# A hybrid decoder layer on one core: conditioning slices regrouped on VectorE, slot arithmetic moved ahead of the first expert, one table load and some dummy matmuls changed

## The reference

```python
c_act = silu(c)
sh1, sc1, gt1, sh2, sc2, gt2 = split(c_act @ w_ada + b_ada, 6)   # six rows of 1024
h = modulate(rmsnorm(x, norm1_g), sh1, sc1)
mix = hybrid_mixer(h, ...)       # 4 GLA heads (two to a unit), 4 HGRN2 heads (one to a unit), chunked
x = x + gt1 * mix
h2 = modulate(rmsnorm(x, norm2_g), sh2, sc2)
ffn = hierarchical_moe(h2, ...)  # 32 experts of width 256, best group of 4, best 2 of its 8 experts
x = x + gt2 * ffn
shf, scf = split(c_act @ w_ada_final + b_ada_final, 2)
out = modulate(rmsnorm(x, norm_f_g), shf, scf)
```

## Time and profile before

| | |
|---|---|
| median of 3 runs | 1039.96 us (1039.79 to 1043.06) |
| profiled execution | 1039.79 us |
| its span, first to last instruction | 1038.0 us |
| PE busy | 981.2 us, 95% |
| PE weight loads | 771.5 us, 74% |
| DVE busy | 797.5 us, 77% |
| ACT busy | 530.4 us, 51% |
| chain that ended last | PE 66%, DVE 15%, DMA 10%, ACT 4%, issue 3% |
| mean granted clock of PE | 0.992 |

### The profile page before, as it was taken

The page is one execution under the profiler, slowest core; times in us unless marked ns, Lnnn a source line. Parts: engine busy times, 40 slices in busy tenths (PEclk is TensorE's granted clock), DMA queues, the critical chain, the costliest instruction groups (busy, mean ns, idle before and its releaser), DMA issues.

```text
span 1038.0 us, 15568 instructions
## 1 busy us (share of the span) xinstructions
PE 981.2 (95%) x5698; PEld 771.5 (74%) x5698; DVE 797.5 (77%) x1486; ACT 530.4 (51%) x930; POOL 109.1 (11%) x151
## 2 busy tenths in 40 slices
PE   5899998999899999999999999899999999999996
PEld 5669688978897998989988888466666666666642
DVE  7859879836983886958676768898888888787828
ACT  4555532654275555555663323465665656565522
POOL 0201101000100000010010000121221221212100
PEclk9899999999999999999999999999999999999998
DMA  9823633232324233230185434589999999999375
GB/s 364 250 80 105 199 105 103 62 101 61 105 61 122 82 93 111 62 102 1 58 333 164 183 141 182 186 292 363 372 370 367 372 366 358 368 355 349 105 306 205
DMA packets 81033, 206.78 MB, mean 199 GB/s; under 512 B 11878, under 2 KB 40630, under 8 KB 72780
## 3 DMA queue, kind: packets, MB, share of 16 engines
q1 hardware_dynamic: 59232, 156.25, 41.8%
q0 software_dynamic: 15120, 43.72, 13.2%
q10 hardware_dynamic: 6620, 6.00, 1.8%
HBM read 189.61 MB, written 24.71 MB: 206 GB/s over the span
## 4 chain that ended last, share of the span: by engine, by line
PE 66%; DVE 15%; DMA 10%; ACT 4%; issue 3%; SPq 1%; ACTq 0%; DVEq 0%; POOLq 0%
PE PS L1999 13%; PE PS L2001 12%; PE PS L2000 12%; DMA WGU<-in_w_exp_up 7%; PE PS L2297 4%; PE PS L2083 3%; PE PS L2305 3%; PE PS L2303 3%; PE PS L2304 3%; DVE AT L1466 3%; PE PS L2288 2%; PE PS L2408 1%; DVE ACC L1264 1%; DMA AST<-in_w_ada 1%; PE PS L2133 1%
## 5 line engine op out<-in xcount | busy, mean ns | idle before, releaser
L1999 PE MATMUL PS<-WH,HT 128*128 128x256 f32 x512 | 146.8, 287 | 1.3 <-ACT GVH L924 1.3
L2000 PE MATMUL PS<-WL,HT 128*128 128x256 f32 x512 | 144.8, 283 | 0.0
L2001 PE MATMUL PS<-WH,HL 128*128 128x256 f32 x512 | 144.8, 283 | 0.0
L1825 DVE TENSOR_TENSOR WGL<-WGU,WGH 128x1024 fp32r<-128x1024 f32 x96 | 116.9, 1219 | 18.1 <-ACT WGH L1171 16.8
L1466 DVE COPY_PREDICATED AT<-MASK,PS 128x64 f32<-128x64 uint8 x320 | 72.8, 228 | 63.1 <-PE PS L2094 44.0
L1171 ACT ACTIVATE WGH<-WGU 128x1024 fp32r<-128x1024 f32 x96 | 98.5, 1064 | 33.6 <-DMA WGU<-in_w_exp_up 28.1
L1999 PEld LDWEIGHTS PS<-WH,HT 128*128 128x128 f32 x512 | 98.2, 192 | 4.0 <-issue 4.0
L2000 PEld LDWEIGHTS PS<-WL,HT 128*128 128x128 f32 x512 | 98.2, 192 | 0.0
L2001 PEld LDWEIGHTS PS<-WH,HL 128*128 128x128 f32 x512 | 98.1, 192 | 0.0
L2303 PE MATMUL PS<-WGH,XGTH 128*96 128x512 f32 x192 | 88.3, 460 | 0.0
L1863 DVE TENSOR_TENSOR WDL<-WDN,WDH 128x2048 fp32r<-128x2048 f32 x32 | 73.4, 2293 | 17.6 <-ACT WDH L1181 17.5
(11 more groups left out here) (355 smaller groups left out, 2259.0 us busy)
## 6 DMA issues: line engine op xcount, KB each, us to landing
WGU<-in_w_exp_gate SPq DMA_DIRECT2D x32, 1024.0 KB, 12.6
WGU<-in_w_exp_up SPq DMA_DIRECT2D x32, 1024.0 KB, 18.5
WDN<-in_w_exp_down SPq DMA_DIRECT2D x32, 1024.0 KB, 13.5
AR<-in_w_ada POOLq DMA_DIRECT2D x32, 512.0 KB, 4.2
WF<-in_w_in SPq DMA_DIRECT2D x28, 512.0 KB, 5.6
AST<-in_w_ada SPq DMA_DIRECT2D x16, 512.0 KB, 8.6
AR<-in_w_ada_final POOLq DMA_DIRECT2D x16, 512.0 KB, 4.7
YG<-expert_rows SPq DMA_DIRECT2D x8, 1024.0 KB, 12.3
```

Source lines behind the costliest of these rows:

```text
L1825: V.tensor_tensor(WGL[s][:, :, ks, :], WGU[s][:, :, ks, :], WGH[(NCH * s + c) % 4][:].bitcast(F32), ALU.subtract).then_inc(wgl_ready, 1)
L1999: MM(ps, wh, xh, start=first, stop=False)
L2000: MM(ps, wh, xl, start=False, stop=False)
L2001: return MM(ps, wl, xh, start=False, stop=last)
```

## The change

Five edits. (1) The slices are regrouped: 5 ahead of the decay, 3 ahead of the five `mul`, 4 inside `remaining(0)`, 4 ahead of the memsets, and 8 instead of 9 in the attention steps of unit 0; the total stays 48. (2) The Silu of one column on ACT is removed. (3) `extra_counts`, `extra_slots` and both picks (now `picked_slots`) stand ahead of the low parts of the first expert's weights; before, the counts and slots stood behind them and the picks inside expert steps 0 and 2. (4) `warm` reads row tile 0 of X1 instead of the last one. (5) The dummy matmuls ahead of the first expert rows are 8 instead of 7, and the 2 behind the transposes of these rows are removed.

```diff
--- before.py
+++ after.py
@@ -142,7 +142,7 @@
     UNIT_ADA = ["gt1", "sh2", "sc2", "gt2", "shf", "scf"]
 
     ROW_STEP = {0: 4, 1: 4}
-    SLICE_STEPS = {0: [1, 5, 5, 9, 9, 11, 11, 13, 13], 1: [5, 5, 9, 9, 11, 11, 13, 13],
+    SLICE_STEPS = {0: [5, 5, 9, 9, 11, 11, 13, 13], 1: [5, 5, 9, 9, 11, 11, 13, 13],
                    2: [0, 1, 6, 7], 3: [0, 1, 6, 7], 4: [], 5: []}
     SLICES_BETWEEN = {2: 4, 3: 4}
 
@@ -1198,7 +1198,6 @@
 
             for part in range(NCH):
                 weights_high(0, 0, part, True)
-            A(TOCK[:], RR[:, 0:1], ACT.Silu)
             rows_high(0, 0, True)
             for s in range(4):
                 expert_step(0, s, True, False)
@@ -1393,7 +1392,7 @@
             link(V.tensor_tensor(LBT[:, 0, :], LBT[:, 0, :], LB[:, 0, :], ALU.subtract))
             V.tensor_tensor(LBT[:, 1, :], LBT[:, 1, :], LB[:, 0, :], ALU.subtract).then_inc(consts, 1)
             lows(0, v_chunks(0))
-            for _ in range(4):
+            for _ in range(5):
                 unit_slice()
 
             def level(ap, s):
@@ -1521,16 +1520,12 @@
             link(V.tensor_scalar(LB[:, 1, :], LB[:, 0, :], -1.0, 1.0, ALU.mult, ALU.add))
             link(V.tensor_scalar(LB[:, 2, :], LB[:, 1, :], -1.0, None, ALU.mult))
             lows(1, k_chunks(1))
-            unit_slice()
             for i in range(NL):
                 sub(0, i)
-                if i in (1, NL - 1):
-                    unit_slice()
-            unit_slice()
+            for _ in range(KD - 5):
+                unit_slice()
             for i in range(NL):
                 mul(0, i)
-            unit_slice()
-
             def remaining(u):
                 sub(u, NL)
                 sub(u, NL + 1)
@@ -1538,23 +1533,21 @@
                     v_.wait_ge(pj_ready, number[("oT", 0, heads(0) - 1, 1)] + 1)
                 sub(u, NL + 2)
                 if u == 0:
-                    unit_slice()
-                    unit_slice()
+                    for _ in range(4):
+                        unit_slice()
                 for i in range(NL, ITEMS):
                     mul(u, i)
-                    if u == 0 and i == NL:
-                        unit_slice()
 
             remaining(0)
             for u in range(UNITS):
                 if is_gla(u):
                     lows(u, g_chunks(u))
+                    for _ in range(4 if u == 0 else 0):
+                        unit_slice()
                     link(V.memset(AT2[:], 0.0))
                     if u == 0:
                         link(V.memset(S[0][64:P], 0.0))
                         link(V.memset(S[1][0:64], 0.0))
-                        for _ in range(3):
-                            unit_slice()
                 later = decay_steps(u + 1) if u + 1 < UNITS else []
                 for n in range(first_step[u], first_step[u + 1]):
                     attention_step(n)
@@ -1737,6 +1730,15 @@
                 link(V.tensor_scalar(IDX[:, 0:NE], EM[0:C, 0, :], float(PAD), None, ALU.add))
                 V.tensor_single_scalar(IDXG[:, 0:NE], IDX[:, 0:NE], PLANE - 1, op=ALU.bitwise_and).then_inc(idxg_ready, 1)
 
+            def picked_slots(hs, dst):
+                for k, mk in enumerate((M1, M2)):
+                    link(V.tensor_tensor(EM[:, hs], SCR[:, hs], mk[:, hs], ALU.mult))
+                    link(V.tensor_reduce(V8[:, 7, hs], EM[:, hs], AX, ALU.add))
+                    last = V.tensor_copy(dst[:, k, hs], V8[:, 7, hs])
+                    if k == 0:
+                        link(last)
+                return last
+
             router_weights()
             v_.wait_ge(gt1_in, 48)
             v_.wait_ge(ios, 12)
@@ -1789,11 +1791,7 @@
                 link(V.tensor_tensor(SCR[:], SCR[:], bc_t(DX[:], NE, NT), ALU.mult))
                 link(V.tensor_tensor(SCR[:], SCR[:], RK[:], ALU.add))
                 link(V.tensor_tensor(SCR[:], SCR[:], bc_t(EC[:], NE, NT), ALU.add))
-
-            def picked_slot(k):
-                link(V.tensor_tensor(EM[:], SCR[:], (M1, M2)[k][:], ALU.mult))
-                link(V.tensor_reduce(V8[:, 7, :], EM[:], AX, ALU.add))
-                link(V.tensor_copy(SLOT[:, k, :], V8[:, 7, :]))
+                link(picked_slots(slice(0, NT), SLOT))
 
             def extra_experts():
                 link(V.tensor_tensor(CMP[:], XINC[0:1, :].rearrange("p (a e) -> p a e", a=1).to_broadcast([1, NX, NE]),
@@ -1870,13 +1868,13 @@
                 if more:
                     weights_low(*after, 2)
 
+            extra_counts()
+            extra_slots()
             for part in range(NCH):
                 weights_low(0, 0, part)
-            extra_counts()
             rows_low(0, 0)
-            extra_slots()
             for s in range(4):
-                expert_step(0, s, True, False, (lambda: picked_slot(s // 2),) if s in (0, 2) else ())
+                expert_step(0, s, True, False)
                 if s == 1:
                     v_.wait_ge(gt2_in, 16)
             with v_.Fori(1, NE // 4 - 1) as it:
@@ -2230,7 +2228,7 @@
 
             def warm(count):
                 for _ in range(count):
-                    MM(WB[0], IDENT[:], X1[:, NT - 1, 0:HALF], start=True, stop=True)
+                    MM(WB[0], IDENT[:], X1[:, 0, 0:HALF], start=True, stop=True)
 
             for kind, i, *part in out_order[1:]:
                 if kind == "rank" and i == 1:
@@ -2278,7 +2276,7 @@
                             last = MM(ps[:, 4 * NE:5 * NE], ONEB[:], MB[:, t * NE:(t + 1) * NE],
                                       start=(t == 0), stop=(t == NT - 1))
                     last.then_inc(pj_ready, 1)
-            warm(7)
+            warm(8)
             evacuated(("lg", NT - 1))
             evacuated(("rank", 1))
 
@@ -2359,7 +2357,6 @@
 
             pe.wait_ge(xg_in[0], 16)
             xg_transposes(0, t_ready)
-            warm(2)
             for s in range(4):
                 expert_step(0, s, True, False)
             with pe.Fori(1, NE // 4 - 1) as it:
```

## The result

The changed kernel takes 1053.39 us (median of 4), the kernel before 1041.28 us beside it: a ratio of 1.0108, 95% interval 1.0092 to 1.0126. It is slower by 1.1%, by 9.6 to 13.1 us as the interval has it. Three executions on record were far longer (1103.92 us here, 1223.93 us beside e1, 5515.1 us in e9); they count in the medians and not in the ratios. The forecast was 1058.0 us with a range of 1048.8 to 1062.4.

A forecast was written before the change was run, and what follows sets the result against it. PE, two thirds of the span, was taken as the bound, with DVE releasing it at both places. 1039.8 plus 9.1 + 3.5 + 2.9 - 1.1 + 0.3 + 3.5 = 18.2 gave 1058.0 us, range 1048.8 to 1062.4.

The forecast's parts named there:

- The slices' waits: Start of unit 0's attention: grouped slices make DVE wait for AR loads, first mask 9.1 us later.
- The clock in unit 0: PE returns at 1.2 GHz after its gap ahead of the second levels: +3.5 us, bounds 0 and 5.0.
- the walk: Slice-by-slice timing of DVE up to unit 0's first mask, giving 139.9 instead of 130.82.
- Small work ahead of the first low parts: Start of the experts: counts, slots and picks on DVE delay PE's transposes by 2.9 us.
- Pick and table load: Expert step 0: ATT 1.1 us earlier without the pick; Silu table load delays the first SIL, +0.3 us.
- The clock at the experts: PE idles 4.4 us ahead of the second transposes, then runs at 1.2 GHz: +3.5 us, up to 5.0.
- The dummies: Ahead of the first expert rows: eighth dummy matmul adds 0.9 us on PE, hidden under DVE; no cost.
- the start of the sum: The profiled execution of the kernel before, 1039.8 us, to which the forecast's terms were added.
- (a): Rival, chance 0.20: waits come but the clock stays up in one or both gaps; 1054.5 or 1051.0 us.
- (b): Rival, chance 0.10: slices' waits mostly hidden, only the experts' start counts; 1041.9 to 1045.4 us.
- (c): Rival, chance 0.05: late expert start taken back by a bound in the later weight stream; 1052.4 us.
- (d): Rival, chance 0.03: faster, slice loads land within about 1 us and gathered rows come after 670; 1039.0 us.

The follow-up runs named there:

- e1: The kernel before with only the slices regrouped: 1049.68 us, ratio 1.0092 to the kernel before.
- e9: The kernel before with the picks in expert steps 2 and 3 and six instead of three dummy matmuls in the gap at the start: 1037.28 us, ratio 0.9968.
- e7: The changed kernel without the loads of slices 4, 7, 10, 11, 14 and 15, all DVE instructions kept: 1041.19 us, ratio 1.0009 to the kernel before.
- e10: The changed kernel without the loads of slices 14 and 15 alone: 1049.00 us, ratio 1.0078 to the kernel before.
- e5: The changed kernel with nine dummy matmuls on PE ahead of unit 0's second levels: 1051.40 us, ratio 1.0101 to the kernel before.
- e2: The kernel before with only counts, slots and both picks moved ahead of the first weights' low parts: 1042.30 us, ratio 1.0020.
- e6: The changed kernel with five dummy matmuls behind the transposes of the first expert's rows: 1051.26 us, ratio 1.0097 to the kernel before.
- e8: The kernel before with its two picks in expert steps 2 and 3 instead of 0 and 2: 1038.76 us, ratio 0.9980.
- e3: The kernel before with only the Silu that pulls the table load ahead removed: 1040.69 us, ratio 1.0002.
- e4: The kernel before with eight dummy matmuls instead of seven, the two behind the first transposes gone, X1 row tile 0 read: 1039.71 us, ratio 0.9994.

## Why the prediction came out right, and what it mis-sized

- *The slices' waits*: predicted +9.1, measured +9.2 (e1: +9.4). Shown to be the waits for AR by e7 and e10. That two slices in a row are free and the next pair waits held, in the places named. That the size is right to 0.1 us is in part luck: the walk has waits of 13.8 us in sum, the trace 14.7, and the wait in the first pair was 0.6 us shorter than in the kernel before (4.35 for 4.93).
- *The clock in unit 0*: predicted 3.5, measured 2.0 (2.4 by e5). Right in mechanism, mis-sized: this term is the step that failed most clearly. I took ten microseconds at 0.50, as in the earlier trace rows, and all of them as work. The low stretch did last 10.2 us, from 136.7 to 146.9, but the fall came in the gap's middle, and PE ran only the last 4.9 us of it.
- *Small work ahead of the first low parts*: predicted +2.9, measured +2.87 (e2: +2.95) against the one trace of the kernel before. Against the other traces without the edit it is down to 1.7, since DVE's wait for WGH, 0.98 us in the one trace that the prediction had, was up to 2.19 us in others, and the small work fills it.
- *Pick and table load*: predicted -1.1 + 0.3 = -0.8. e6, in which the clock is up, gives 8.91 - 9.79 = -0.9; e8 gives the pick alone, -1.13, and so the load +0.25. The page of the Trainium skill "ScalarE: Activation LUTs", "What ACT_TABLE_LOAD costs", gives 2.66 us a switch, by which, as an estimate, the first SIL would be 2.3 us late. The trace shows 1.28 us and the activation 0.01 us behind it (687.57, 688.86); in e3 the distance to the turn did not change. The measurement decides: here no drain shows between the load and the activation.
- *The clock at the experts*: predicted 3.5, measured 0.49 + 0.88 = 1.4. Mis-sized too, but otherwise than in unit 0: the clock fell at about 679.4, just as PE came back, and was up again by 682.9, so the low stretch lay wholly on work but was 3.4 us long and not ten. Its length is not fixed: it was 6.8 us at the same place in e5 and e10, and 6.8 (e6, e10) and 13.7 us (e1) in unit 0. That the gap brings the clock down is shown by e6. The Trainium skill, "TensorE: Matmul & The Clock Gate", part 1, has the throttled state as the default, lifted by activity; the trace of unit 0 agrees, with 0.50 from 136.7 us, while PE was idle, and 1.00 from 146.9, while it worked.
- *The dummies*: predicted nothing, measured 0.1 (e4).

The sum of the measured terms is 9.2 + 2.0 + 2.9 + 0.5 = 14.6 us, where 0.5 holds pick, load and clock. The pair of traces differs by 12.5. The rest is the start, 70.88 - 69.26 = 1.6 us in the changed kernel's favour, which no edit touches, and 0.5 us between the mixer and the router, from the eighth levels to IDXG (481.22 against 481.75), a distance that lies between 480.8 and 482.8 in the twelve traces. The forecast was 4.6 us too high against the median. The change itself was forecast at 18.2 us and measured at 12.1 by medians, 6.1 too high; the 1.5 us between the two come from the start of the sum, 1039.8, which lies below the median of 1041.28 beside the changed kernel. Of the 6.1 us, 3.6 are the two clock terms. The rest is not pinned down: the pair of traces puts it on the start and the stretch ahead of the router, e2 and e7 on the small work. That the measured time lies in the range owes something to its width of 13.6 us.

Of the rivals, (a) was the nearest in time but not in mechanism: the clock fell in both gaps. (b) was refuted by e1; (c) by the same distance from the first turn to the end (360.7 us in both traces, though it lies between 359.5 and 362.2 in the twelve); (d) by the waits of 3 to 4 us.

## What to carry to other kernels

With two buffers, count how many consumers stand in a row in the engine's order: here two were free, and the one after them waited 2.8 to 4.3 us, for a load that could be issued only when the first of the two was used. Spread them evenly. Small work that is needed late does not belong ahead of the first operand that PE waits for, and not just ahead of a product that PE waits for either. And when a stall on TensorE grows, add the clock that comes after it, but count only the low stretch that falls on work (here it cost 0.4 us for each of its microseconds, 2.0 for 4.9 and 1.4 for 3.4); where PE has to wait behind that work anyway, it is free.

## What was unexpected of the hardware

- The granted clock fell after a gap of 2.05 us (e4), and in e9 twice with less: at 34 us, with 0.61 us of idle ahead of a row of one-column matmuls, and at 126 us behind 0.81 us, where e8 with the same gap kept its clock. In the kernel before it fell with 3.14 us of idle. The gap's length alone does not tell whether it falls.
- PEclk and the durations of the matmuls disagree in one place: in e7 the matmuls from 23.6 to 31.8 us took nearly twice their usual time while PEclk read 1.00. Both are worth reading.
- The low clock at the start goes with 3 us of scatter between executions: the first slice starts at 67.9 to 68.0 us where the mean clock over 31 to 41 us was 1.00 or 0.83, at 69.3 to 69.6 where it was 0.66, and at 70.5 to 70.9 where it was 0.50 to 0.54, in twelve traces. It is as large as some effects measured here, so single traces were compared by distances within them. Distances scatter too, by 1.2 us from IDXG to the second transposes.
